# Forming the low half of one weight sum on VectorE instead of GpSimd, in a two-layer encoder kernel

## What is computed

```python
hf = rmsnorm(x, g_pre_ffn)
f = (jax.nn.silu(hf @ w_gate) * (hf @ w_up)) @ w_down
return x + rmsnorm(f, g_post_ffn)
```

## Time and profile before

| | us |
|---|---|
| median of three runs | 3127.76 |
| the runs | 3125.1, 3127.76, 3127.8 |
| profiled execution, its own time | 3123.86 |
| profiled execution, span of its instructions | 3122.0 |
| PE busy | 3061.8 (98%) |
| DVE busy | 1951.6 (63%) |
| ACT busy | 1125.9 (36%) |
| POOL busy | 1034.2 (33%) |

### The profile page before, as it was taken

How to read it: one execution, slowest core, us unless ns; L and a number is a source line. 1 busy time by engine, 2 the same in 40 slices (tenths; PEclk the granted TensorE clock), 3 DMA queues, 4 the chain that set the end, 5 groups by cost and what they waited for, 6 DMA issues and landing times.

```text
span 3122.0 us, 48846 instructions
## 1 busy us (share of the span) xinstructions
PE 3061.8 (98%) x19092; PEld 2800.2 (90%) x19092; DVE 1951.6 (63%) x3698; ACT 1125.9 (36%) x2117; POOL 1034.2 (33%) x801
## 2 busy tenths in 40 slices
PE   9999999999999999999999999999999999999997
PEld 7888887999999999888888888879999999998886
DVE  6866656388744446666587666573887444576565
ACT  5433444454322224212354344444533222341111
POOL 1211211665522235212542111127555222461112
PEclk9999999999999999999999999999999999999998
DMA  4111011333322234222231110123232222332223
GB/s 152 45 56 51 19 40 53 112 106 113 98 68 67 67 113 139 100 85 111 95 118 38 53 50 25 34 63 120 97 121 81 71 78 69 126 136 91 91 76 120
DMA packets 116563, 261.23 MB, mean 84 GB/s; under 512 B 12272, under 2 KB 64624, under 8 KB 116080
## 3 DMA queue, kind: packets, MB, share of 16 engines
q1 hardware_dynamic: 114032, 250.24, 24.1%
q10 hardware_dynamic: 2304, 7.87, 0.6%
HBM read 192.52 MB, written 57.67 MB: 80 GB/s over the span
## 4 chain that ended last, share of the span: by engine, by line
PE 89%; DVE 5%; issue 2%; DMA 1%; POOL 1%; ACT 1%; SPq 1%; DVEq 0%; POOLq 0%; ACTq 0%
PE PS L2217 27%; PE PS L2219 26%; PE PS L2218 26%; PE PS L2369 4%; PE PS L2338 3%; PE PS L2353 2%; PE PS L2255 1%; DVE PT L1962 1%; POOL OSS L1029 1%; DVE ACC L1675 1%; DVE ACC L1673 0%; PE PS L2313 0%; DMA EB<-rpb 0%; ACT PT L1354 0%; DMA EYE<-small 0%
## 5 line engine op out<-in xcount | busy, mean ns | idle before, releaser
L2217 PE MATMUL PS<-XH,WH 128*128 128x512 f32 (+1 forms) x1152 | 433.1, 376 | 14.2 <-DVE Rv L1836 4.5
L2219 PE MATMUL PS<-XH,WL 128*128 128x512 f32 (+1 forms) x1152 | 409.8, 356 | 0.0
L1018 POOL TENSOR_TENSOR WL<-RAW,WH 128x1024 fp32r<-128x1024 f32 x105 | 258.1, 2468 | 455.3 <-ACT WH L1231 455.3
L2218 PE MATMUL PS<-XL,WH 128*128 128x512 f32 (+1 forms) x1152 | 408.6, 355 | 0.0
L2015 DVE TENSOR_TENSOR ACC<-ACC,PS 128x512 f32<-128x512 f32 (+1 forms) x432 | 253.4, 597 | 223.0 <-PE PS L2219 222.3
L2217 PE MATMUL PS<-HH,WH 128*128 128x512 f32 (+1 forms) x1056 | 377.7, 358 | 2.0 <-DVE HL L1796 2.0
L2219 PE MATMUL PS<-HH,WL 128*128 128x512 f32 (+1 forms) x1056 | 376.8, 357 | 0.0
L2218 PE MATMUL PS<-HL,WH 128*128 128x512 f32 (+1 forms) x1056 | 376.7, 357 | 0.0
L1051 POOL TENSOR_TENSOR GL<-GR,GH 128x512 fp32r<-128x512 f32 x186 | 252.2, 1369 | 361.6 <-ACT GH L1397 300.7
L2217 PEld LDWEIGHTS PS<-XH,WH 128*128 128x128 f32 x1152 | 217.4, 189 | 72.1 <-issue 18.8
L1962 DVE TENSOR_TENSOR PT<-PS,PT 128x512 fp32r<-128x512 f32 (+1 forms) x328 | 165.4, 537 | 165.1 <-ACT PT L1354 162.3
(11 more groups left out here) (206 smaller groups left out, 7912.8 us busy)
## 6 DMA issues: line engine op xcount, KB each, us to landing
GR<-w_gu SPq DMA_DIRECT2D x62, 768.0 KB, 4.3
HF<-hidden SPq DMA_DIRECT2D x44, 640.0 KB, 6.6
RAW<-w_in SPq DMA_DIRECT2D x48, 512.0 KB, 3.7
RAW<-w_down SPq DMA_DIRECT2D x44, 512.0 KB, 4.4
GR<-w_gu SPq DMA_DIRECT2D x62, 256.0 KB, 2.8
hidden<-S1T SPq DMA_DIRECT2D x44, 192.0 KB, 1.9
hidden<-U2T SPq DMA_DIRECT2D x44, 192.0 KB, 1.9
RAW<-w_out SPq DMA_DIRECT2D x16, 512.0 KB, 4.6
```

Of the source, the lines that this page charges most:

```text
L1018: nc.gpsimd.tensor_tensor(WL[s][:, :, :], RAW[s][:, :, :], WH[s][:, :, :].bitcast(F32), ALU.subtract).then_inc(s_lo, 1)
L2217: nc.tensor.matmul(out, wh, xh, start=first, stop=False, skip_group_check=reopened)
L2218: nc.tensor.matmul(out, wh, xl, start=False, stop=False, skip_group_check=reopened)
L2219: return nc.tensor.matmul(out, wl, xh, start=False, stop=last, skip_group_check=reopened)
```

## The change

The name S4 joins the list of low halves that DVE forms (`LOW_V`), the semaphore of POOL's S4 is gone, and POOL's `weight_sum_low` with its two calls is removed. DVE forms the low half of S4 as the third of the three behind gate1, ahead of up2; for visit 0 it is the fourth of four beside the output projection. The counts of DVE's semaphore go from three to four a visit.

```diff
-LOW_V = ("S2", "S3", "S1")
+LOW_V = ("S2", "S3", "S1", "S4")
...
-            def weight_sum_low(L, v):
-
-                m = BLOCK["S4"]
-                pool.wait_ge(s_whi, high_weights(L, v, "S4"))
-                pool.wait_ge(s_wsum, summed_weights(L, v, "S4"))
-                nc.gpsimd.tensor_tensor(GL[v % 2][:, m, :, :], GR[v % 2][:, m, :, :],
-                                        GH[v % 2][:, m, :, :].bitcast(F32), ALU.subtract).then_inc(s_wlo_s4, 1)
...
                             for name in RAW_ORDER:
                                 raw_low(L, 0, name)
-                            weight_sum_low(L, 0)
...
                         raw_low(L, v + 1, "A12")
-                        weight_sum_low(L, v + 1)
...
                     if v > 1:
-                        dve.wait_ge(s_wlo_v, 3 * VISIT[L, v] - 3)
+                        dve.wait_ge(s_wlo_v, 4 * VISIT[L, v] - 4)
...
-                dve.wait_ge(s_wsum, summed_weights(L, v, "S4" if name == "S2" else "S2" if name == "S1" else "S3"))
+                dve.wait_ge(s_wsum, summed_weights(L, v, "S4" if name in ("S2", "S4") else "S2" if name == "S1" else "S3"))
...
                     if prepare:
                         weight_sum_low(L, v + 1, "S3")
                         weight_sum_low(L, v + 1, "S1")
+                        weight_sum_low(L, v + 1, "S4")
...
-                    elif name in LOW_V:
-                        pe.wait_ge(s_wlo_v, 3 * VISIT[L, v] - 2 + LOW_V.index(name))
                     else:
-                        pe.wait_ge(s_wlo_s4, VISIT[L, v])
+                        pe.wait_ge(s_wlo_v, 4 * VISIT[L, v] - 3 + LOW_V.index(name))
```

More of the change, by code:

```diff
@@ L597, in build @@
         s_wlo_v = sem("wlo_v")
-        s_wlo_s4 = sem("wlo_s4")
         s_xn = sem("xn")
```

## The result

| | before | with the change |
|---|---|---|
| median, us (20 runs each) | 3126.28 | 3131.81 |
| lowest and highest run, us | 3122.59 to 3127.89 | 3128.83 to 3134.55 |
| span of the profiled execution, us | 3122.0 | 3129.0 |
| DVE busy, us | 1951.6 | 1964.3 |
| POOL busy, us | 1034.2 | 949.2 |

The ratio is 1.0019, with a 95% interval of 1.0012 to 1.0026: the kernel is slower by 0.19 in a hundred, some 5.9 us (0.0019 x 3126; the medians lie 5.5 us apart). The time of 3131.81 us is inside the stated range, but the rise is more than twice the +2.5 us of the forecast.

A forecast was written before the change was run, and what follows sets the result against it. PE, busy 98%, was taken as the bound, so moved work costs only where PE waits. Turn 9 gave 2 x 1.25 = +2.5 us, all else 0: 3127.76 + 2.5 = 3130.3 us, range 3124 to 3135.5.

The forecast's parts named there:

- What bounds it, and the price: PE busy 98%, so DVE time costs only where PE waits; a low half costs 0.6 us with POOL idle.
- Narrow turns: Narrow single turns: up2, hid1 and hidden2 move back 0.6 us, DVE's idle 1.20 us before u2 takes it; cost 0.
- the prediction's own signs of being wrong: A new PE wait in narrow turns or at turn 0, or a wait at turn 10 that is not longer.
- Wide single turns: Wide turns 1 to 8: the added 0.6 us ahead of up2 is covered by idle time or existing waits; cost 0.
- Beside the output projection: Visit 0: an added low half priced 0.6 to 1.85 us, with 0.97 us of cover before turn 0; taken as 0.
- Turn 9: DVE waits for two long POOL instructions instead of one, making u2 later by 1.25 us a layer.
- the help of turn 8: POOL's shorter turn 8 brings work for turn 9 about 0.45 us earlier; without it +1.70 us a layer.
- (a): Turn 9: T1 starts behind the S4 low half, so no cost or small gain, 3127.8 or 3126.5 us; chance 0.22.
- (b): Turn 9: POOL keeps the port between T1 and T4, +7.4 us in all, 3135.2 us; chance 0.10.
- (c): Something not seen, anywhere in the kernel; chance 0.06, half of it slower by more than 0.2%.
- no new wait of PE elsewhere: Sign of being right: PE waits longer only for u2 of turn 10, about 1.9 us a layer against 0.6.
- the 5.2 us: Upper bound on the cost: 3.4 us from turn 9 without turn 8's help, 5.2 with the output projection.

The follow-up runs named there:

- turns 2 and 4 on POOL: Against the change, POOL forms the low half of S4 again in turns 2 and 4; PE's u3 waits went from 3.4 us to 0.
- turns 3 and 5 on POOL: Against the change, POOL forms the low half of S4 again in turns 3 and 5; PE's u3 waits stayed at 3.4 us.
- the run without the port: Kernel before, with DVE's low half of S1 (value from PSUM, no port needed) made twice; ratio 1.0020.
- the change in four turns alone: Kernel before, with S4's low half moved to DVE only in turns 2, 4, 9 and 41 of each layer; ratio 1.0031.

## Why the prediction was right in range and short in size

- **What bounds it, and the price.** Right. The moved work costs only where PE waits for it. A free low half with two SBUF inputs took 0.67 to 0.69 us. The median of 146 is 0.68 where it was 1.31 of 84, mostly because 58 of the 62 added ones took under 0.70 us; the 60 behind gate1 went from 1.32 to 1.08, since POOL is less in the way. One reading of the rows was off: POOL's low half in the earlier trace rows ends 1.17 us behind the end of DVE's (1160.79 less 1159.62), where the prediction has 1.29. Nothing hangs on it. DVE's busy time rose by 12.7 us and POOL's fell by 85.
- **Narrow turns.** Right for u2: 0.63 us of idle time is left of 1.20, as forecast. Wrong for turn 41, and with it one of the prediction's own signs of being wrong came, a new PE wait in the narrow turns: the step "up2, hid1 and POOL's hidden2 move back 0.6 us" was written down and then costed at nothing, without asking what is queued behind hidden2 on POOL. It is the down weights' low half, and it costs 0.9 us.
- **Wide single turns: this is the step that failed.** I wrote that the steps of the norm follow, that DVE has 0.95 us of idle time before the next u2, and "Cost 0". The idle time covers DVE's own next instruction, not ACT, which waits for the last norm step, nor POOL's fold behind ACT. That is 3.4 of the 6.1 us, shown by turns 2 and 4 on POOL (0) against turns 3 and 5 on POOL (3.4), and by the run without the port.
- **Beside the output projection.** Right: no wait of PE at turn 0 in the trace. The low half of B11 ends at 690.19 and PE starts turn 0 at 691.47, a cover of 1.28 us where 0.97 was read.
- **Turn 9.** The mechanism was right in each step, the sum of +2.5 us was too high: measured +1.8. About half of the miss is the help of turn 8, put at 0.45 us a layer and measured as 0.64. The other half is in the steps themselves: without that help (the change in four turns alone) the wait rose by 3.0 us, where the working had 3.4.
- **The rivals.** (a) did not happen: T1 starts ahead of the added low half. (b) did not happen: DVE got the port between T1 and T4. What came was (c), the one that I had not seen, on top of the forecast: 4.3 of the 6.1 us of new waits were not in the working. Of the signs of the prediction's last part, "no new wait of PE elsewhere" failed.
- **Luck.** The forecast of 3130.3 us lies only 1.5 us under the measured median because it was counted from a median of three runs, 3127.76, which lay 1.5 us above that of twenty. And the rise of 5.5 us is more than the 5.2 us that the working gives as its bound; the range reached further for (b), whose mechanism did not occur.

## What to carry to other kernels

Idle time behind an added instruction covers the engine's own next instruction only. For each result that comes later, ask who waits for it on another engine, what is queued behind that on this engine, and which port or order it then meets: here two engines further on and one turn later. And look at the order of two contenders, not at the sum of their times: an instruction of 0.6 us moved POOL's fold from just ahead of DVE's first sum to just ahead of the second. POOL then had its next instruction ready right behind the fold, and DVE met two of POOL's instructions where it had met one.

## What the runs showed of the hardware that was not expected

A delay on DVE of 0.6 us made PE wait 1.2 us in turn 3, twice its own size. In turn 5 it was 0.6 us. It didn't matter whether the delaying instruction used the shared port (u3 waits of 3.4 us) or not (3.3 us). The exclusion of DVE and POOL for whole instructions multiplies small shifts: which of two starts first by some tenths of a microsecond (0.13 us before, 0.26 us with the change) decides whether a DVE sum takes 0.7 us or 2.8 to 2.9. The Trainium skill has this in one sentence, that the order of issue and not the form of the instruction decides who blocks ("SBUF — State Buffer", section "Who interferes with whom"); the trace agrees, with the S1 sum at 2.83 us before and the S3 sum at 2.90 with the change, for the same fold. The traces show one thing more, who comes next when both engines have an instruction waiting. In turn 9 of all eleven traces a DVE low half that was waiting got in between POOL's T1 and T4, though T4 was ready behind T1: the two took 5.64 to 6.19 us together, where 2 x 2.40 would be 4.80. With the change that kept DVE's wait to two of POOL's long instructions, where rival (b) had three.
